# RWKV token matrices of every second pair of heads in exchanged partition halves, so that a product set addresses all four array quarters

## The chip, the cores and the metric

One core of one Trainium2 chip runs the whole program. The metric is the device time of one execution in microseconds (us); lower is better.

## The reference, cut to what matters

The program is one inference step of a two-layer network. The change lies in the RWKV-7 time mixing of the first layer, for 640 tokens (512 latent, 128 context), 8 heads of 64, in both directions of time. Per head and direction it computes

```
def rwkv7_recurrence(r, decay, kk, b, k, v, s0):
    def step(s, inp):
        r_t, w_t, kk_t, b_t, k_t, v_t = inp
        sa = einsum('dbhvk,dbhk->dbhv', s, kk_t)
        s = s * w_t[..., None, :] - sa[..., :, None] * b_t[..., None, :] + v_t[..., :, None] * k_t[..., None, :]
        return s, einsum('dbhvk,dbhk->dbhv', s, r_t)
```

All inputs and outputs are float32.

## The kernel before

The recurrence is done in chunks of 64 tokens. The 640 tokens are five tiles of 128; a **turn** (`n`, five of them) takes one tile in each direction (`e` = 0 forward, 1 backward). 128 partitions hold a pair of heads, 64 partitions each, so a direction has four pairs (`c`, RC = 4) of two chunks each (`u`): eight blocks (`j = 2c + u`, RB = 8), and a block has two independent 64x64 matrices, one in either partition half (`HALVES`).

A **product set** is 16 products of 64x64 by 64x64, one per block and half. The helper `each` (L1124) multiplies two tiles block by block, `turned` (L1134) transposes by a product with the identity `half_ident`, `added` (L1209) sums three products. Half 0 reads partitions 0 to 63 and writes partitions 0 to 63 of a PSUM bank, half 1 reads and writes 64 to 127. On the 128x128 array that is two of the four 64x64 quarters, those on the diagonal. Each float32 product appears in the trace as two MATMUL records and two LDWEIGHTS records, so a set is 32 MATMUL records.

The order of work is written out by hand, one function per engine, with semaphores between them: `rwkv_pe`, `rwkv_act`, `rwkv_dve`, `rwkv_pool`. A turn on TensorE has three stretches.

1. **Opening.** Four pair products per direction (B by A, K by A, B by R, K by R), the transposes of A, B, K, V and of the masked matrix Lm, and M by V. ScalarE copies each PSUM bank out (`LT`, `AMV`, `Btok`, `Ktok`, `Vtok`); VectorE masks the others (`MT`, `TbT`, `TkT`; L1313, L1320, L1323), makes `Lm` (`mask_level`, L1295), `XT` (L1309) and `X` (L1316).
2. **Levels.** Five rounds (`for lv in range(1, LEVELS)`) of Lm by X, XT by T1 and T1 by XT, with the low-rank products of the next turn (`prepare_lora_pe`) between them.
3. **End.** XT by AMV (L1196, 128 columns), two sets with nWG (`Phi`, `Hm`), then in two steps the new state and the output: state of both directions (first `added` loop), output of both directions (second), for step 0 and then for step 1, whose state `Sc1` VectorE makes from step 0's products (L1356).

VectorE also prepares the next turn between these: the running sums (L1053 to L1063) after `Hm`, whose exponentials ScalarE takes (L1069 to L1072), A (L1077), and, after the outputs are added into `yT` (L1365), R (L1080). Then come six small operations on the decays `em` (L1298 to L1300), `Sc` (L1303) and the first masks. GpSimd makes B and K of the next turn (L1085 to L1094) and adds the bonus; TensorE's first product of a turn waits for A, B and K of both directions (`tile_ready`).

Ahead of the turns the state is brought into place by eight transposes (L996), after them it is turned back by eight (L1393).

Of the kernel before, what the change touches and what calls it, by code (L numbers as in the profile page):

```python
# [12 lines left out]
P = 128  # L13
# [102 lines left out]
def build(nc, i, o):  # L116

    ctx = ExitStack()
    with ctx:
# [826 lines left out]
        em, em_now = [wr(RB) for _ in BOTH], [wr(RB) for _ in BOTH]  # L946
# [44 lines left out]
        def rwkv_state_pe(pe):  # L991
            pe.wait_ge(sem("lora_in"), 48)
            pe.wait_ge(sem("state_in"), 32)
            for e in range(2):
                for c in range(RC):
                    last = nc.tensor.transpose(ps[e][:, c * N:(c + 1) * N], stin[:, e, 2 * c:2 * c + 2, :].rearrange("p h k -> p (h k)"),  # L996
                                               ident[0:N, 0:N])
            last.then_inc(sem("state_turned"), 1)
# [26 lines left out]
        def bank(b):  # L1025
            return ps[b][:, :].rearrange("p (b t) -> p b t", b=RB)

# [84 lines left out]

        def rwkv_pe(pe):
            for e in BOTH:
                if e:
                    pe.wait_ge(sem("a_made"), 1)
                prepare_lora_pe(0, e, pe)
            for n in range(NT):
# [17 lines left out]

                pe.wait_ge(sem("tile_ready"), n * 4 + 4)
                for e in BOTH:
                    each(4 * e + 1, Bst[e], Ast[e]).then_inc(sem("pairs_done"), 1)
                for e in BOTH:  # L1140
                    turned(4 * e + 2, blocks_of(Ast[e])).then_inc(sem("abk_turned"), 1)
                for e in BOTH:
                    pe.wait_ge(sem("rwkv_y_kept"), n * 2 + (e + 1))
                    each(4 * e, Kst[e], Ast[e]).then_inc(sem("pairs_done"), 1)
                for e in BOTH:
                    turned(4 * e + 3, blocks_of(Bst[e])).then_inc(sem("abk_turned"), 1)
# [3 lines left out]
                for e in BOTH:  # L1150
                    pe.wait_ge(sem("abk_kept"), n * 6 + (e + 1))
                    turned(4 * e + 2, blocks_of(Kst[e])).then_inc(sem("abk_turned"), 1)
                for e in BOTH:
                    pe.wait_ge(sem("abk_kept"), n * 6 + (e + 3))
                    turned(4 * e + 3, tile_blocks(V0, n, e)).then_inc(sem("v_turned"), 1)
                for e in BOTH:
                    pe.wait_ge(sem("m_kept"), n * 2 + (e + 1))
                    pe.wait_ge(sem("r_made"), n * 2 + (e + 1))
                    each(4 * e, Bst[e], Rst[e]).then_inc(sem("pairs_done"), 1)
                for e in BOTH:  # L1160
                    pe.wait_ge(sem("abk_kept"), n * 6 + (e + 5))
                    each(4 * e + 2, Kst[e], Rst[e]).then_inc(sem("pairs_done"), 1)
# [4 lines left out]
                for lv in range(1, LEVELS):  # L1167
                    for e in BOTH:
                        pe.wait_ge(sem("x_updated"), n * 2 * (LEVELS - 1) + (2 * (lv - 1) + e + 1))
                        pe.wait_ge(sem("level_masked"), n * 2 * LEVELS + (2 * lv + e + 1))  # L1170
                        each(4 * e + 1, Lm[e], X[e]).then_inc(sem("lx_done"), 1)
                    if lv == 1 and n + 1 < NT:
                        pe.wait_ge(sem("incl_kept"), n * 4 + 2)
                        prepare_lora_pe(n + 1, 0, pe)
                    if lv == 3 and n + 1 < NT:
                        pe.wait_ge(sem("a_made"), n * 2 + 3)
                        prepare_lora_pe(n + 1, 1, pe)
                    for e in BOTH:
                        if lv == 1:
                            pe.wait_ge(sem("incl_kept"), n * 4 + (e + 3))  # L1180
                            pe.wait_ge(sem("mv_kept"), n * 2 + (e + 1))
                        pe.wait_ge(sem("lx_kept"), n * 2 * (LEVELS - 1) + (2 * (lv - 1) + e + 1))
                        pe.wait_ge(sem("xt_updated"), n * 2 * LEVELS + (2 * (lv - 1) + e + 1))
                        if lv < LEVELS - 1:
                            each(4 * e + 2, XT[e], T1[e]).then_inc(sem("x_product"), 1)
                        else:
                            each(4 * e + 3, T1[e], XT[e]).then_inc(sem("xt_product"), 1)
                    if lv < LEVELS - 1:
                        for e in BOTH:
                            each(4 * e + 3, T1[e], XT[e]).then_inc(sem("xt_product"), 1)  # L1190

                for e in BOTH:
# [6 lines left out]
                if n + 1 < NT:  # L1199
                    pe.wait_ge(sem("a_made"), n * 2 + 4)  # L1200
                for e in BOTH:
                    pe.wait_ge(sem("wg_kept"), n * 2 + (e + 1))
                    each(4 * e, nWG[e][:, :, 0:N], Btok[e])
                    each(4 * e + 3, nWG[e][:, :, 0:N], TbT[e]).then_inc(sem("phi_done"), 1)
# [6 lines left out]

                for step in range(2):
                    state = Sc1 if step else Sc
                    for e in BOTH:
                        u = 1 - e if step else e
                        pe.wait_ge(sem("sc_made" if step else "phi_kept"), n * 2 + (e + 1))
# [12 lines left out]
        def rwkv_act(act):  # L1229
            for e in BOTH:  # L1230
# [4 lines left out]
                prepare_exps_act(0, e, act)  # L1235
            for n in range(NT):
                for e in BOTH:
                    act.wait_ge(sem("pairs_done"), n * 8 + (e + 1))
                    nc.scalar.copy(LT[e], bank(4 * e + 1)).then_inc(sem("lt_kept"), 1)
                for e in BOTH:  # L1240
                    act.wait_ge(sem("abk_turned"), n * 6 + (e + 1))
                    nc.scalar.copy(AMV[e][:, :, 0:N], bank(4 * e + 2)).then_inc(sem("abk_kept"), 1)
                for e in BOTH:
                    act.wait_ge(sem("abk_turned"), n * 6 + (e + 3))
                    nc.scalar.copy(Btok[e], bank(4 * e + 3)).then_inc(sem("abk_kept"), 1)
                for e in BOTH:
                    act.wait_ge(sem("abk_turned"), n * 6 + (e + 5))
                    nc.scalar.copy(Ktok[e], bank(4 * e + 2)).then_inc(sem("abk_kept"), 1)
                for e in BOTH:
                    act.wait_ge(sem("v_turned"), n * 2 + (e + 1))  # L1250
                    nc.scalar.copy(Vtok[e], bank(4 * e + 3)).then_inc(sem("v_kept"), 1)
# [20 lines left out]
                for e in BOTH:  # L1272
                    act.wait_ge(sem("wg_done"), n * 2 + (e + 1))
# [3 lines left out]
                if n + 1 < NT:  # L1277
                    prepare_exps_act(n + 1, 1, act)

        def rwkv_dve(dve):  # L1280
# [8 lines left out]
            for n in range(NT):  # L1289
# [7 lines left out]
                for e in BOTH:  # L1297
                    nc.vector.tensor_copy(em_now[e], em[e])  # L1298
                    nc.vector.tensor_scalar(em_kept[e], sub_cols(em[e], e), keep[:, ds(n, 1)], None, ALU.mult)
                    nc.vector.tensor_tensor(em_pair[e], sub_cols(em[e], 0), sub_cols(em[e], 1), ALU.mult)  # L1300
# [10 lines left out]
                for e in BOTH:  # L1311
                    dve.wait_ge(sem("pairs_done"), n * 8 + (e + 3))
                    nc.vector.tensor_tensor(MT[e], bank(4 * e), bc(strict[:, e * N:(e + 1) * N], [P, RB, N], 1), ALU.mult).then_inc(sem("m_kept"), 1)  # L1313
                for e in BOTH:
# [3 lines left out]
                for e in BOTH:  # L1318
                    dve.wait_ge(sem("pairs_done"), n * 8 + (e + 5))
                    nc.vector.tensor_tensor(TbT[e], bank(4 * e), bc(within[:, e * N:(e + 1) * N], [P, RB, N], 1), ALU.mult).then_inc(sem("incl_kept"), 1)  # L1320
                for e in BOTH:
                    dve.wait_ge(sem("pairs_done"), n * 8 + (e + 7))
                    nc.vector.tensor_tensor(TkT[e], bank(4 * e + 2), bc(within[:, e * N:(e + 1) * N], [P, RB, N], 1), ALU.mult).then_inc(sem("incl_kept"), 1)  # L1323
# [22 lines left out]
                for e in BOTH:  # L1346
                    dve.wait_ge(sem("phi_done"), n * 2 + (e + 1))
                    nc.vector.tensor_tensor(Phi[e], bank(4 * e), eye, ALU.add)
                    nc.vector.tensor_tensor(Hm[e], bank(4 * e + 3), Rst[e], ALU.add)
# [9 lines left out]
                for e in BOTH:  # L1359
                    dve.wait_ge(sem("state_made"), n * 4 + (e + 3))  # L1360
                    nc.vector.tensor_tensor(S[e], sub(bank(4 * e), 1 - e), bc(sub_cols(em_now[e], 1 - e), [P, RC, N], 2), ALU.mult)
                for e in BOTH:
                    y = yT[:, :, tokens_of(n, e)]
                    dve.wait_ge(sem("y_done"), n * 2 + (e + 1))
                    nc.vector.tensor_tensor(y, y, ps[4 * e + 3][:, :].rearrange("p (c t) -> p c t", c=RC), ALU.add)  # L1365
# [22 lines left out]
        def rwkv_end_pe(pe):  # L1388
            end_step_pe(pe, 0, lambda c: pairs, lambda c: yT[:, c, :])

            for e in range(2):
                for c in range(RC):
                    last = nc.tensor.transpose(ps[4 + e][0:N, c * P:(c + 1) * P], S[e][:, c, :], ident)  # L1393
# [1005 lines left out]
```

## Time and profile before

| | us |
|---|---|
| three runs: median (lowest to highest) | 2692.62 (2692.33 to 2698.26) |
| profiled execution: its own time | 2691.81 |
| profiled execution: span | 2689.8 |
| TensorE busy in the span | 2448.0 (91%) |
| VectorE / ScalarE / GpSimd busy | 601.4 / 536.0 / 217.9 |
| the five turns, first product to the last output | 457.55 to 796.26 |

The span runs from the first to the last instruction; the execution's own time is 2.0 us longer. A busy time is the union of an engine's records. A matrix product's record is longer than the time after which the next may start, so rates are taken from counts over a stretch and not from the mean of one record. The granted TensorE clock is given as a share of 2.4 GHz: 1.00 is 2.4, 0.50 is 1.2.

### The profile page before, as it was taken

What the parts mean: (1) busy time and instruction counts of PE and PEld (TensorE: products, weight loads), DVE (VectorE), ACT (ScalarE), POOL (GpSimd) and SP (SyncE); (2) the same over time, 40 slices, a digit from 0 to 9 for tenths busy, and PEclk for the clock granted to TensorE, in tenths of its full rate; (3) what the DMA queues carried; (4) which work ended last, traced back from release to release, by engine and by line L of the source; (5) the groups of instructions that cost most, each with busy time, mean ns of one, the idle gap of its engine ahead of it and who ended that gap; (6) DMA issues with size and microseconds to landing.
All of it is one profiled execution on the core that took longest, in us unless ns stands there. A gap on an engine that the chain in (4) does not pass through costs nothing.

```text
span 2689.8 us, 74227 instructions
## 1 busy us (share of the span) xinstructions
PE 2448.0 (91%) x34058; PEld 1706.7 (63%) x34058; DVE 601.4 (22%) x1164; ACT 536.0 (20%) x1037; POOL 217.9 (8%) x243
## 2 busy tenths in 40 slices
PE   5899985999999769999999899998794999999998
PEld 3555564999994466777666345457453777766654
DVE  1113456666652330000000010106315000000001
ACT  3111043444421310000000036114413000000000
POOL 2000020333300010000000000003001000000000
PEclk8999997999999889999999999999896999999999
DMA  7665300000012269999999311110014999999970
GB/s 282 191 216 180 132 1 14 4 4 4 4 44 68 108 248 373 397 397 396 396 394 392 115 50 47 48 63 32 16 58 159 353 392 397 396 394 394 396 274 39
DMA packets 173468, 529.19 MB, mean 197 GB/s; under 512 B 23124, under 2 KB 27888, under 8 KB 173296
## 3 DMA queue, kind: packets, MB, share of 16 engines
q1 hardware_dynamic: 158688, 489.45, 48.1%
q10 hardware_dynamic: 10336, 24.21, 3.1%
q0 software_dynamic: 4272, 12.91, 1.4%
q8 instruction: 147, 2.41, 0.4%
q14 instruction: 25, 0.20, 0.0%
HBM read 506.75 MB, written 11.40 MB: 193 GB/s over the span
## 4 chain that ended last, share of the span: by engine, by line
PE 68%; issue 16%; DMA 5%; DVE 3%; ACT 2%; POOLq 1%; ACTq 1%; DVEq 1%; POOL 1%; SPq 0%
PE ps L1710 19%; PE ps L1725 17%; PE ps L1124 7%; PE ps L458 4%; PE ps L1840 4%; DMA big<-w_exp_down 3%; PE ps L1209 2%; PE ps L1912 2%; PE ps L1134 2%; PE ps L1908 2%; PE ps L460 1%; PE ps L830 1%; PE ps L438 1%; PE ps L1703 1%; PE ps L1196 1%
## 5 line engine op out<-in xcount | busy, mean ns | idle before, releaser
L1710 PE MATMUL ps<-rs,ring 128*64 128x80 f32 x12288 | 441.8, 233 | 5.8 <-issue 5.5
L1710 PEld LDWEIGHTS ps<-rs,ring 128*64 128x64 f32 x12288 | 429.9, 137 | 23.9 <-issue 23.0
L1811 DVE TENSOR_TENSOR big<-big,ps 128x320 f32<-128x320 f32 x64 | 28.3, 483 | 993.8 <-PE ps L1725 954.8
L1725 PE MATMUL ps<-big 128*80 128x512 f32 x512 | 226.4, 595 | 1.9 <-DMA big<-w_exp_down 1.5
L1725 PE MATMUL ps<-ring,big 128*80 128x512 f32 x512 | 225.0, 592 | 2.4 <-DVE big L1811 2.4
L555 PE MATMUL ps<-hT,ring 128*128 128x512 f32 x336 | 176.1, 606 | 11.1 <-ACTq L602 11.1
L1124 PE MATMUL ps<-big 64*64 64x64 f32 x5440 | 166.5, 219 | 16.9 <-DVEq L1095 16.9
L1781 ACT COPY big<-ps 80x512 f32<-80x512 f32 x64 | 34.1, 582 | 711.0 <-PE ps L1725 711.0
L1124 PEld LDWEIGHTS ps<-big 64*64 64x64 f32 x5440 | 163.1, 136 | 18.2 <-DVEq L1095 17.2
L1725 PEld LDWEIGHTS ps<-ring,big 128*80 128x80 f32 x512 | 76.6, 150 | 145.9 <-issue 141.8
L1725 PEld LDWEIGHTS ps<-big 128*80 128x80 f32 x512 | 74.3, 150 | 131.5 <-issue 129.8
L1710 PE MATMUL ps<-rs,big 128*64 128x80 f32 x4096 | 148.2, 233 | 1.6 <-issue 1.6
L1710 PEld LDWEIGHTS ps<-rs,big 128*64 128x64 f32 x4096 | 144.5, 137 | 2.6 <-issue 2.4
L1912 PE MATMUL ps<-hT,ring 128*128 128x512 f32 x256 | 132.0, 597 | 0.8 <-issue 0.8
L1840 PE MATMUL ps<-hT,big 128*128 128x512 f32 x256 | 115.1, 602 | 3.4 <-DMA prompt_rows<-big 3.4
L556 PEld LDWEIGHTS ps<-hT,ring 128*128 128x128 f32 x336 | 64.4, 192 | 81.6 <-issue 81.6
L458 PE MATMUL ps<-hT,ring 128*128 128x512 f32 x192 | 100.4, 605 | 10.5 <-issue 9.3
L1743 POOL COPY rs<-big 128x640 f32 (+1 forms) x32 | 23.1, 722 | 928.9 <-PE ps L1710 928.9
L1913 PEld LDWEIGHTS ps<-hT,ring 128*128 128x128 f32 x256 | 48.6, 190 | 61.2 <-issue 61.2
L1840 PEld LDWEIGHTS ps<-hT,big 128*128 128x128 f32 x256 | 48.6, 195 | 59.8 <-issue 55.3
L1774 ACT ACTIVATE big<-ps 128x320 f32<-128x320 f32 x64 | 24.5, 435 | 288.8 <-PE ps L1710 288.8
L1908 PE MATMUL ps<-ring,hT 128*128 128x512 f32 x160 | 69.2, 593 | 0.3 <-issue 0.3
(392 smaller groups left out, 3002.1 us busy)
## 6 DMA issues: line engine op xcount, KB each, us to landing
ring<-w_exp_up SPq DMA_DIRECT2D x124, 1024.0 KB, 10.8
ring<-w_exp_gate SPq DMA_DIRECT2D x68, 1024.0 KB, 12.1
big<-w_exp_down SPq DMA_DIRECT2D x64, 1024.0 KB, 11.3
ring<-w_exp_down SPq DMA_DIRECT2D x64, 1024.0 KB, 11.5
big<-w_exp_gate SPq DMA_DIRECT2D x60, 1024.0 KB, 10.6
big<-w_ada SPq DMA_DIRECT2D x22, 2048.0 KB, 8.7
ring<-w_in_odd SPq DMA_DIRECT2D x6, 2048.0 KB, 8.9
big<-big ACTq DMA_DIRECT2D x32, 256.0 KB, 6.4
```

Source lines behind the costliest of these rows:

```text
L458: nc.tensor.matmul(ps[2 * pair][:, :], blocks[s][:, k, j * P:(j + 1) * P], rhs(k, 0, TS), start=(k == 0), stop=(k == KC - 1))
L555: nc.tensor.matmul(ps[2 * pair][:, :], w, hT[:, k, 0:TS], start=(k == 0), stop=(k == KC - 1))
L556: last = nc.tensor.matmul(ps[2 * pair + 1][:, 0:TP], w, hT[:, k, TS:T], start=(k == 0), stop=(k == KC - 1))
L1124: last = nc.tensor.matmul(ps[b][hf, j * N:(j + 1) * N], lhs[hf, j, :], rhs[hf, j, :], start=True, stop=True)
L1134: last = nc.tensor.matmul(ps[b][hf, j * N:(j + 1) * N], x[j][hf], half_ident[hf, :], start=True, stop=True)
L1209: last = nc.tensor.matmul(ps[b][hf, j * N:(j + 1) * N], lhs[hf], rhs[hf], start=(t == 0), stop=(t == len(terms) - 1))
L1710: last = nc.tensor.matmul(ps[2 * m + j // 4][a:a + HALF, (j % 4) * SLOTS:(j % 4 + 1) * SLOTS], ex_blocks[ex_slot(q)][:, k % 2, j * P + a:j ...
L1725: last = nc.tensor.matmul(ps[4 + f][0:SLOTS, :], hid[:, k, :], ex_blocks[ex_slot(q)][:, k % 2, f * W:(f + 1) * W], start=(k == 0), stop=(k ...
L1840: nc.tensor.matmul(ps[b][:, :], outS[:, a, c * P:(c + 1) * P], turnS[:, a, :], start=(a == 0), stop=(a == E // 2 - 1))
L1908: last = nc.tensor.matmul(ps[2 * pair][:, :], hT[:, k, tile * P:(tile + 1) * P], blocks[s][:, k, :], start=(k == 0), stop=(k == KC - 1))
L1912: nc.tensor.matmul(ps[2 * pair][:, :], w, hT[:, k, 0:TS], start=(k == 0), stop=(k == KC - 1))
L1913: last = nc.tensor.matmul(ps[2 * pair + 1][:, 0:TP], w, hT[:, k, TS:T], start=(k == 0), stop=(k == KC - 1))
```

## The change

For odd pairs `c` the two heads' token matrices (what has tokens on its partitions, or results from such) exchange partition halves. Even pairs keep the diagonal quarters, odd pairs read half g and write half 1 - g, which are the other two quarters. The new helper `across` goes through four places `k` and takes in each an even pair (f = 0, bank b) and an odd pair (f = 1, bank b + 1), so four products in a row address four quarters. `added_across` does it for the outputs. The sets that go through them, per direction and turn: four pair products, the transposes of A, B, K and V, and the outputs (three sets). `each`, `turned` and `added` keep the others: Lm's transpose, M by V, the levels, XT by AMV, `Phi`, `Hm` and the states.

Since a set now fills half of two banks, the readers take both (`spread`), and the results stand in order of place (`placed`). The pair products, transposes and outputs share banks in a new order: the transposes of A, B, K and V all use banks 4e+2 and 4e+3, the pair products banks 4e and 4e+1, each waiting until the one before has been read. Three things are added: R is moved to exchanged halves by a set of products with the identity and copied to `Hm` by ScalarE before XT by AMV (`r_turned`, `r_placed`); the decays `em` of odd pairs cross halves by two products of 64x4 and two copies per direction (`place_em_pe`, `place_em_act`), for the next turn ahead of the step 1 outputs; and the state goes in and out by 16 products in place of eight transposes each.

On TensorE, the opening of the first turn. Before (L1124 is `each`, L1134 `turned`; two sets of 16 per pair of rows):

```order
L1124 MATMUL ps<-big 64x64 [waits tile_ready]
L1124 MATMUL ps<-big 64x64 x31
L1134 MATMUL ps<-big 64x64 x32
L1124 MATMUL ps<-big 64x64 [waits rwkv_y_kept]
L1124 MATMUL ps<-big 64x64 x15
L1124 MATMUL ps<-big 64x64 [waits rwkv_y_kept]
L1124 MATMUL ps<-big 64x64 x15
L1134 MATMUL ps<-big 64x64 x32
L1134 MATMUL ps<-big 64x64 [waits level_masked]
```

and with the change (L1175 is `across`, L1164 `turned`):

```order
L1175 MATMUL ps<-big 64x64 [waits em_placed,tile_ready]
L1175 MATMUL ps<-big 64x64 x15
L1175 MATMUL ps<-big 64x64 [waits em_placed]
L1175 MATMUL ps<-big 64x64 x15
L1175 MATMUL ps<-big 64x64 [waits rwkv_y_kept]
L1175 MATMUL ps<-big 64x64 x15
L1175 MATMUL ps<-big 64x64 [waits rwkv_y_kept]
L1175 MATMUL ps<-big 64x64 x15
L1164 MATMUL ps<-big 64x64 [waits level_masked]
```

Eight sets stood ahead of the one that waits for the mask of Lm; four are left. K by A and the transpose of B now follow it.

On VectorE, the opening of the first turn. Before:

```order
L1303 TENSOR_TENSOR big<-big 128x256 x2
L1295 TENSOR_TENSOR big<-big 128x512 [waits lt_kept] x2
L1309 TENSOR_TENSOR big<-big 128x512 x2
L1313 TENSOR_TENSOR big<-ps,big 128x512 [waits pairs_done] x2
```

and with the change, where L1388 is `X`, L1369 `mask_level`, and L1392 `MT` (L1313 before):

```order
L1378 TENSOR_TENSOR big<-big 128x256 x2
L1369 TENSOR_TENSOR big<-big 128x512 [waits lt_kept] x2
L1384 TENSOR_TENSOR big<-big 128x512 x2
L1388 TENSOR_TENSOR big<-big,ps 128x512 [waits x_product]
L1369 TENSOR_TENSOR big<-big 128x512
L1388 TENSOR_TENSOR big<-big,ps 128x512 [waits x_product]
L1369 TENSOR_TENSOR big<-big 128x512
L1392 TENSOR_TENSOR big<-ps,big 128x512 [waits pairs_done] x2
```

`MT` went behind both `X` and their masks.

On TensorE, the start of the end stretch with the change (L1250 is XT by AMV, L1196 before); the first two rows are the new set of R, for both directions:

```order
L1175 MATMUL ps<-ring0,big 64x64 [waits a_made]
L1175 MATMUL ps<-ring0,big 64x64 x31
L1250 MATMUL ps<-big 64x128 [waits r_placed,xt_updated]
L1250 MATMUL ps<-big 64x128 x15
```

Before, XT by AMV waited for `xt_updated` alone, and `a_made` was waited for behind it.

The diff, cut to its core:

```
+        def spread(b):
+            return banks[:, b * 512:(b + 2) * 512].rearrange("p (f r) -> p f r", f=2)[:, :, 0:4 * N].rearrange("p f (k t) -> p f k t", k=4)
...
+        def place_em_pe(turn, pe):
+            for e in BOTH:
+                pe.wait_ge(sem("exps"), turn * 2 + (e + 1))
+                odd_pairs = em[e].rearrange("p (a f u) -> p f a u", a=2, f=2)[:, 1]
+                for g in range(2):
+                    last = nc.tensor.matmul(ps[4 * e + 1][HALVES[1 - g], 0:4].rearrange("p (a u) -> p a u", a=2), half_ident[HALVES[g], :],
+                                            odd_pairs[HALVES[g]], start=True, stop=True)
+                last.then_inc(sem("em_crossed"), 1)
...
+                def across(b, lhs, rhs, apart=1):
+
+                    for k in range(4):
+                        for f in range(2):
+                            for g in range(2):
+                                last = nc.tensor.matmul(ps[b + apart * f][HALVES[g ^ f], k * N:(k + 1) * N], half_ident[HALVES[g], :] if lhs is None else lhs[f][k][HALVES[g]],
+                                                        half_ident[HALVES[g], :] if rhs is None else rhs[f][k][HALVES[g]], start=True, stop=True)
+                    return last
...
                 for e in BOTH:
-                    each(4 * e + 1, Bst[e], Ast[e]).then_inc(sem("pairs_done"), 1)
-                for e in BOTH:
-                    turned(4 * e + 2, blocks_of(Ast[e])).then_inc(sem("abk_turned"), 1)
+                    if n:
+                        pe.wait_ge(sem("sc_made"), n * 4 + (e - 1))
+                    pe.wait_ge(sem("em_placed"), n * 2 + (e + 1))
+                    across(4 * e, b_of[e], a_of[e]).then_inc(sem("pairs_done"), 1)
...
+                for e in BOTH:
+                    across(4 * e, None, r_of[e], 2).then_inc(sem("r_turned"), 1)
                 for e in BOTH:
                     pe.wait_ge(sem("xt_updated"), n * 2 * LEVELS + (2 * (LEVELS - 1) + e + 1))
+                    pe.wait_ge(sem("r_placed"), n * 2 + (e + 1))
...
+                    if step and n + 1 < NT:
+                        place_em_pe(n + 1, pe)
                     for e in BOTH:
                         u = 1 - e if step else e
-                        for c in range(RC):
-                            j = 2 * c + u
-                            last = added(4 * e + 3, j, [(Vtok[e][:, j], TkT[e][:, j]), (nWG[e][:, j, N:P], TbT[e][:, j]), (state[e][:, c], Hm[e][:, j])])
+                        for a in range(2):
+                            k = 2 * a + u
+                            last = added_across(4 * e + 2, k, [(two(Vtok[e], k), two(TkT[e], k)), (two(nWG[e][:, :, N:P], k), two(TbT[e], k)),
+                                                               ([state[e][:, 2 * f + a] for f in range(2)], two(Hm[e], k))])
...
                 for e in BOTH:
+                    act.wait_ge(sem("r_turned"), n * 2 + (e + 1))
+                    for f in range(2):
+                        last = nc.scalar.copy(Hm[e][:, 4 * f:4 * f + 4, :], ps[4 * e + 2 * f][:, 0:4 * N].rearrange("p (k t) -> p k t", k=4))
+                    last.then_inc(sem("r_placed"), 1)
```

## Rows read from the trace of the kernel before

**Rows 1.** Windows of three stretches; columns: us, engines' busy us, clock, DMA.

```profile
457.50:463.60 6.10, 6.05 (x114) 6.05 (x116) 5.15 (x14) 1.77 (x3) 0.00 (x0) 0.50 0.01 4
595.90:614.60 18.70, 18.70 (x648) 18.70 (x645) 13.33 (x25) 6.48 (x11) 2.73 (x2) 1.00 0.02 4
614.60:645.00 30.40, 30.40 (x934) 30.02 (x930) 20.86 (x31) 16.46 (x34) 13.58 (x11) 1.00 0.02 4
```

**Rows 2.** Timeline, TensorE, one turn: start us, duration us, then line and operands.

```profile
595.93 2.03 PE L1124 MATMUL ps<-big 64*64 64x64 f32 x64
...
614.60 2.03 PE L1124 MATMUL ps<-big 64*64 64x64 f32 x64
```

**Rows 3.** Window of line L351 alone; groups of the list by line.

```profile
37.10:40.50 3.40, 3.40 (x128) 3.27 (x132) 1.00 0.08 8
...
L1710 PE MATMUL ps<-rs,ring 128*64 128x80 f32 x12288 | 441.8, 233 | 5.8 <-issue 5.5
...
L1725 PE MATMUL ps<-big 128*80 128x512 f32 x512 | 226.4, 595 | 1.9 <-DMA big<-w_exp_down 1.5
...
L810 PE MATMUL ps<-big 64*128 64x384 f32 x32 | 7.9, 573 | 0.5 <-ACTq L868 0.5
```

**Rows 4.** Timeline, TensorE, end of a turn; last row: window, line L1209.

```profile
577.20 3.74 PE L1196 MATMUL ps<-big 64*64 64x128 f32 x64
...
584.50 0.28 PE L1209 MATMUL ps<-ring 64*64 64x64 f32 x4
...
584.50:595.93 11.43, 11.41 (x384) 11.27 (x384) 1.00 0.02 4
```

**Rows 5.** Timeline, ScalarE: state-in copies, the turn's end, the next turn's first copy.

```profile
425.99 0.65 ACT L1003 COPY big<-ps 128x256 f32<-128x256 f32 x2 [0.82 <-PE ps L996]
...
576.00 1.15 ACT L1047 ACTIVATE ring<-ps,parB 128x128 f32<-128x128 f32 x4
...
597.08 0.59 ACT L1239 COPY big<-ps 128x512 f32<-128x512 f32 x1 [6.11 <-PE ps L1124]
```

**Rows 6.** Timeline, VectorE and GpSimd between two turns.

```profile
589.25 0.76 DVE L1356 TENSOR_TENSOR big<-ps,big 128x256 f32<-128x256 f32 x2
...
592.80 1.27 POOL L1094 TENSOR_TENSOR big<-ring 128x512 f32<-128x512 f32 x1
```

**Rows 7.** Timeline, VectorE, start of a turn.

```profile
596.15 0.69 DVE L1365 TENSOR_TENSOR hT<-hT,ps 128x512 f32<-128x512 f32 x1 [0.71 <-PE ps L1209]
...
600.64 1.29 DVE L1295 TENSOR_TENSOR big<-big 128x512 f32<-128x512 f32 x2
602.03 1.30 DVE L1309 TENSOR_TENSOR big<-big 128x512 f32<-128x512 f32 x2
```

**Rows 8.** Windows of a later stage with waits; columns as in rows 1.

```profile
1852.70:1856.20 3.50, 1.71 (x8) 1.53 (x9) 2.26 (x5) 3.25 (x8) 0.00 (x0) 1.00 0.00 0
1869.80:1873.30 3.50, 0.21 (x1) 0.21 (x2) 2.77 (x5) 2.10 (x5) 1.10 (x1) 1.00 0.02 7
1873.30:1876.70 3.40, 3.40 (x9) 2.69 (x9) 3.21 (x5) 1.34 (x4) 1.90 (x1) 0.50 0.00 0
```

**Rows 9.** Timeline, first turn: TensorE, then VectorE.

```profile
457.55 3.68 PE L1124 MATMUL ps<-big 64*64 64x64 f32 x64 [16.89 <-DVEq L1095]
...
461.02 3.19 PE L1134 MATMUL ps<-big 64*64 64x64 f32 x64
...
478.98 2.03 PE L1124 MATMUL ps<-big 64*64 64x64 f32 x64
...
461.75 1.28 DVE L1295 TENSOR_TENSOR big<-big 128x512 f32<-128x512 f32 x2
```

**Rows 10.** Timeline, VectorE and TensorE around the stage's two edges.

```profile
426.34 4.33 DVE L1006 MEMSET hT<- 128x5120 f32 x1 [1.26 <-PEq L186]
...
787.17 0.43 DVE L1356 TENSOR_TENSOR big<-ps,big 128x256 f32<-128x256 f32 x1 [1.20 <-PE ps L1209]
...
801.10 1.04 PE L1393 MATMUL ps<-ck,big 128*64 128x128 f32 x8
```

More of the change, by code:

```diff
@@ L945, in build @@
         half, go_on = wr(RB), wr(1)
-        em, em_now = [wr(RB) for _ in BOTH], [wr(RB) for _ in BOTH]
+        em, em_placed, em_now = ([wr(RB) for _ in BOTH] for _ in range(3))
         em_kept, em_pair = [wr(RC) for _ in BOTH], [wr(RC) for _ in BOTH]
@@ L995, in rwkv_state_pe @@
                 for c in range(RC):
-                    last = nc.tensor.transpose(ps[e][:, c * N:(c + 1) * N], stin[:, e, 2 * c:2 * c + 2, :].rearrange("p h k -> p (h k)"),
-                                               ident[0:N, 0:N])
+                    for h in range(2):
+                        q = 2 * (c % 2) + c // 2
+                        last = nc.tensor.matmul(ps[e][HALVES[h ^ (c % 2)], q * N:(q + 1) * N], stin[:, e, 2 * c + h, :], ident[0:N, 0:N], start=True, stop=True)
             last.then_inc(sem("state_turned"), 1)
@@ L1158, in rwkv_pe @@
                     pe.wait_ge(sem("r_made"), n * 2 + (e + 1))
-                    each(4 * e, Bst[e], Rst[e]).then_inc(sem("pairs_done"), 1)
+                    across(4 * e, b_of[e], r_of[e]).then_inc(sem("pairs_done"), 1)
                 for e in BOTH:
                     pe.wait_ge(sem("abk_kept"), n * 6 + (e + 5))
-                    each(4 * e + 2, Kst[e], Rst[e]).then_inc(sem("pairs_done"), 1)
+                    across(4 * e + 2, heads(tile_blocks(V0, n, e)), None).then_inc(sem("v_turned"), 1)
+                for e in BOTH:
+                    pe.wait_ge(sem("incl_kept"), n * 4 + (e + 1))
+                    across(4 * e, k_of[e], r_of[e]).then_inc(sem("pairs_done"), 1)
                 for e in BOTH:
@@ L1198, in rwkv_pe @@
                     last.then_inc(sem("wg_done"), 1)
-                if n + 1 < NT:
-                    pe.wait_ge(sem("a_made"), n * 2 + 4)
                 for e in BOTH:
                     pe.wait_ge(sem("wg_kept"), n * 2 + (e + 1))
-                    each(4 * e, nWG[e][:, :, 0:N], Btok[e])
-                    each(4 * e + 3, nWG[e][:, :, 0:N], TbT[e]).then_inc(sem("phi_done"), 1)
+                    each(4 * e + 1, nWG[e][:, :, 0:N], Btok[e])
+                    each(4 * e + 2, nWG[e][:, :, 0:N], TbT[e]).then_inc(sem("phi_done"), 1)
                 def added(b, j, terms):
@@ L1210, in added, with added_across, two @@
                     return last
+                def added_across(b, k, terms):
+                    for t, (lhs, rhs) in enumerate(terms):
+                        for f in range(2):
+                            for g in range(2):
+                                last = nc.tensor.matmul(ps[b + f][HALVES[g ^ f], k * N:(k + 1) * N], lhs[f][HALVES[g]], rhs[f][HALVES[g]],
+                                                        start=(t == 0), stop=(t == 2))
+                    return last
+                def two(x, k):
+                    return [x[:, 4 * f + k] for f in range(2)]
                 for step in range(2):
@@ L1215, in rwkv_pe @@
                         u = 1 - e if step else e
-                        pe.wait_ge(sem("sc_made" if step else "phi_kept"), n * 2 + (e + 1))
+                        pe.wait_ge(sem("sc_made" if step else "phi_kept"), n * (4 if step else 2) + (e + 1))
                         for c in range(RC):
@@ L1272, in rwkv_act @@
                 for e in BOTH:
+                    act.wait_ge(sem("r_turned"), n * 2 + (e + 1))
+                    for f in range(2):
+                        last = nc.scalar.copy(Hm[e][:, 4 * f:4 * f + 4, :], ps[4 * e + 2 * f][:, 0:4 * N].rearrange("p (k t) -> p k t", k=4))
+                    last.then_inc(sem("r_placed"), 1)
+                for e in BOTH:
                     act.wait_ge(sem("wg_done"), n * 2 + (e + 1))
@@ L1392, in rwkv_end_pe @@
                 for c in range(RC):
-                    last = nc.tensor.transpose(ps[4 + e][0:N, c * P:(c + 1) * P], S[e][:, c, :], ident)
+                    q = 2 * (c % 2) + c // 2
+                    for h in range(2):
+                        last = nc.tensor.matmul(ps[4 + e][0:N, c * P + h * N:c * P + (h + 1) * N], S[e][:, q, :],
+                                                ident[:, HALVES[h ^ (c % 2)]], start=True, stop=True)
             last.then_inc(sem("state_turned"), 1)
```

69 lines of the change are left out of this document (45 added, 24 removed).

## The prediction

> **What bounds the kernel now.** I read the windows by stage first, then TensorE's timeline, then the engines it waits for. Inside the turns TensorE never stops: 18.70 us busy of 18.70 in the opening of a turn and 30.40 of 30.40 in the levels, at the full clock [rows 1]. An opening is 20 product sets from 595.93 to 614.60 [rows 2], so a set of 32 records takes 18.67 / 20 = 0.933 us, 58 ns for every two records, one in either quarter of the diagonal. The reader should see that nothing else limits this: VectorE is busy 13.33 of the 18.70 us and ScalarE 6.48 [rows 1]. TensorE's time is thus the stage's time, but the cover is thin: VectorE makes its first mask of the turn only at 600.64, 4.7 us after the first product [rows 2, 7], and that wait is hidden by sets that the change shortens or moves.
>
> **Does a quarter cost nothing beside another?** The trace has no stretch with four 64x64 quarters, so the price of an `across` set has to be bounded. A full row of 512 columns takes 226.4 / 512 = 0.442 us, so 64 columns stream in 55 ns, hardly less than the 58 seen for two records. Line L351, which writes four groups of partitions, starts 128 records of 128 columns in 3.40 us, 26.6 ns each, where one alone streams 110 ns: four go on at once, from the same input partitions. L1710 does the same with two groups and 64-column weight loads: 36 ns a record where 80 columns stream 69. L810 reads the two halves of the input and writes the same 128 output partitions, in two banks: 7.9 us / 32 = 247 ns where 384 columns stream 331 [rows 3]. Both directions of sharing are there, not their product. The low bound of a set is therefore 0.467 us (four records in 58 ns), the high bound 0.933 (no gain). I take 0.467, since each of the two sharings alone costs nothing in its row.
>
> The Trainium skill, "TensorE: Matmul & The Clock Gate", Part 3, says that a weight load overlaps running products only where its row group differs; two of the four quarters share theirs. By that rule a set would stay near 0.933. L1710's 36 ns, with both column groups on all rows, speaks against it [rows 3].
>
> **The change, part by part.** Times from here count from the start of the state products, 584.50, called P.
>
> *Set of R, before XT by AMV.* The `a_made` it waits for ends at 577.15, XT by AMV began at 577.20 [rows 4, 5]. R of both directions takes 577.2 to 578.15. ScalarE starts 0.22 after the first direction's set (as 597.08 stands to 596.86 [rows 2, 5]) and copies two pieces of 256 columns, priced at 0.65 by the copies at 425.99 [rows 5]: done at 578.55. XT by AMV then starts at 578.65, **1.45 us later**; the second direction's copies lie under the first's product. P moves with it.
>
> *Outputs and states.* Twelve sets took 11.43 us [rows 4]. State step 0 stays: 3.03 with its short wait. Step 0's outputs shrink from 2.8 to 1.4 and end at P + 4.43. There a wait appears: `Sc1` of the first direction is ready only at 589.25 + 0.43 = P + 5.18 [rows 6, 10], as VectorE does the running sums first. State step 1 runs 5.25 to 8.05, the crossing of `em` 0.2 (the exponentials are ready by about P + 6.5, since GpSimd starts behind them), step 1's outputs to 9.65. B and K of the next turn are ready when GpSimd's L1094 ends, 594.07 = P + 9.57, some 0.1 later with its drain [rows 6]. The turn starts at **P + 9.75** instead of 11.43.
>
> *The opening.* Product B by A and the transpose of A are four short sets: to P + 11.6. Lm's transpose then waits for the mask. VectorE adds the last outputs 0.22 after them, and from that addition (596.15) to the end of the first mask (600.64 + 0.69) takes 5.18 [rows 7]: 9.65 + 0.22 + 5.18 = 15.05. **TensorE idles 3.5 us.** From there: Lm 15.1 to 16.95, transposes of B to 17.9. VectorE ends `XT` 2.69 after the mask began [rows 7], at 17.05, then makes X, mask, X, mask in steps of 0.6 to 0.65, to 19.6. K by A goes at 17.9 and, behind the second X, at 19.1 to 19.55; K's transposes to 20.5; `MT` is kept at 20.2 and 20.85; B by R 20.5 to 21.4, V to 22.3, K by R (behind `TbT`, 21.85 and 22.5) to 23.3, M by V, two full sets, to 25.1. The levels start at **P + 25.1**; before, at 614.60 - 584.50 = 30.1. So a boundary gains 5.0 - 1.45 = 3.5 us. The levels themselves keep 30.40: their sets stay.
>
> *The clock.* In a later stage a stretch with TensorE busy 0.21 of 3.50 us was followed by one at 0.50 of the clock (1.2 GHz); one with 1.71 of 3.50 was not [rows 8]. An idle 3.5 us lies between. I take a fall at nearly every boundary and a return soon after: at half the clock two sets take 461.02 - 457.55 = 3.47 us [rows 9], so Lm's pair takes 3.4 instead of 1.87, of which VectorE's chain absorbs about 0.8: 0.7 lost. A boundary nets 2.8, four of them **11.2 us**.
>
> *First turn.* From 457.55 to 478.98 before [rows 9], beginning at half the clock [rows 1]. The masks start at 461.75 as now [rows 9]; Lm at 462.5, at half the clock to 465.9, then B's transposes, K by A at 467.8. With the clock back about then, `MT` ends at 469.6 and the levels follow 4.3 later as above: 473.9. Half of that clock's return is open, so I take **4.5** of the 5.
>
> *Last turn.* The wait for R costs 1.45, the outputs give back 2.8; `Sc1` is ready at 787.60 [rows 10], under the products: **1.35**.
>
> *State in and out.* Eight transposes become 16 products. Inbound they lie under VectorE's 4.33 us fill [rows 10]; without that cover they cost 1 us. Outbound they stand on TensorE's path: eight took 0.87, 32 records one after another take 1.85: **-1.0**.
>
> *At nothing:* the `em` copies (ScalarE waited 6.11 us for its first copy of a turn [rows 5]); reading two banks in place of one, as the elements stay 512. If that cost an operation 0.17 us (half-size operations take 0.43 each [rows 10] against 0.69 [rows 7]), five on the chain would take 0.9 a turn; both ends go into the range.
>
> Sum: 11.2 + 4.5 + 1.35 - 1.0 = 16.0 us. The profiled execution took 2691.81, 0.8 under the median of the runs: **2676 us**.
>
> **The rivals.**
>
> *The issue of records is the limit.* No stretch starts records faster than the 26.6 ns of L351 [rows 3]; a short set needs 14.6. If 26.6 is as fast as they can be issued, a set takes 0.85 us. Outputs end at P + 11.13, the mask at 16.5, and behind Lm come twelve sets of 0.85 and M by V: levels at P + 30.5, 0.4 later than now, and R delays P by 1.85. Each boundary loses 2.25, the last turn 1.35, the state out 1.0: **2703, slower**. It decides above about 0.7 us a set, where gain and loss meet. Against it: L351's rate is explained by its columns. Chance 0.15. The Trainium skill, same page, "Back-to-back issue gap", gives a floor of about 25 ns from start to start for small products; by that, an estimate, a set would take 0.8 us. The trace neither reaches nor breaks it.
>
> *The quarters don't overlap.* A set stays 0.933, and only the new waits and sets remain: 3.8 a boundary, 2711. Against it all of [rows 3]. Chance 0.05.
>
> *Partial overlap,* 0.7 us a set: levels at P + 28, R 1.65, so 0.45 a boundary gained and eaten by the state out: 2690. Chance 0.10.
>
> *The clock stays low* through most of each opening: 2.5 lost a boundary instead of 0.7 and 2 more in the first turn: 2685. For it: sparse work after the gap. Against: from K by A on TensorE is nearly dense. Chance 0.10.
>
> **How the numbers follow.** The forecast has 0.60: 2671 (no fall of the clock, first turn 6) to 2681 (two-bank reads at their bound). A difference under 0.3%, 8 us, can't be told from none. Faster: the forecast and half of the low clock, 0.65; same: the other half, the partial case and a milder issue limit, 0.17; slower: the rest, 0.18. The range takes in the forecast, the low clock and the partial case with their bounds, 2668 to 2697.
>
> **What would show it.** `across` sets with 32 records in about 0.47 us; an idle stretch of some 3.5 us on TensorE after the transposes of A, ended by VectorE's first mask, and the clock at 0.50 behind it; XT by AMV waiting about 0.5 us for ScalarE; turns of 64 to 65 us instead of 67.8. Wrong it would be if 32 records took 0.8 us or more, if K by A rather than Lm waited longest, or if the next turn's B and K came later than 9.7 us after the state products began.

## The result, and the profile after

The changed kernel takes 2695.93 us (median of 20 runs, 2689.82 to 2702.50), the kernel before 2689.53 us beside it (20 runs, 2685.02 to 2698.26): a ratio of 1.0025, 95% interval 1.0017 to 1.0033. So it is slower by a quarter of a per cent, 6.4 us, where 2676 was forecast. The time lies inside the range, near its upper end, but the forecast had the direction wrong. The profiled execution took 2697.08 us.

The page, engines and the queue of instructions, changed kernel (each engine: busy us, share of the span, instructions):

```profile
span 2695.3 us, 75088 instructions
...
PE 2425.0 (90%) x34466; PEld 1674.0 (62%) x34466; DVE 602.8 (22%) x1164; ACT 542.6 (20%) x1077; POOL 219.0 (8%) x243
...
q8 instruction: 150, 2.46, 0.4%
```

TensorE is busy 23 us less than before (2448.0) and the span is 5.5 us longer, so its idle time over the span grew by some 28 us. Window of the turns, from the first pair product to the pass that follows them (columns as in [rows 1]):

```profile
457.54:802.98 345.44, 306.49 (x11041) 298.79 (x11041) 210.47 (x346) 133.46 (x278) 101.48 (x88) 0.97 0.02 4
```

Before, the same stretch (457.55 to 796.44) took 338.89 us, 337.87 of them busy. The array was relieved as meant, by 31 us here; but where TensorE idled 1 us it now idles 39, and the turns take 6.55 us more. Starts of XT by AMV, in us:

| turn | 1 | 2 | 3 | 4 | 5 |
|---|---|---|---|---|---|
| before | 509.38 | 577.20 | 645.00 | 712.82 | 776.62 |
| after | 509.73 | 578.65 | 649.66 | 719.08 | 784.44 |

The turns that should have shrunk from 67.8 to 64 or 65 us take 68.9, 71.0, 69.4 and, the last, 65.4 (63.8 before). At the last XT by AMV the kernel is 7.8 us late.

TensorE's timeline in one opening, changed kernel (it answers to [rows 2]; at the end of a line the idle time before it, and what released it):

```profile
526.71 0.73 PE L1175 MATMUL ps<-big 64*64 64x64 f32 x33
528.23 1.62 PE L1175 MATMUL ps<-big 64*64 64x64 f32 x95 [0.79 <-issue]
532.74 2.02 PE L1164 MATMUL ps<-big 64*64 64x64 f32 x62 [2.88 <-DVE big L1369]
...
536.72 1.63 PE L1175 MATMUL ps<-big 64*64 64x64 f32 x96 [0.50 <-DVE big L1388]
538.17 0.65 PE L1175 MATMUL ps<-ring,big 64*64 64x64 f32 x32
540.25 0.69 PE L1175 MATMUL ps<-ring,big 64*64 64x64 f32 x32 [1.44 <-issue]
540.77 1.11 PE L1175 MATMUL ps<-big 64*64 64x64 f32 x64
541.70 0.65 PE L1175 MATMUL ps<-ring,big 64*64 64x64 f32 x32
543.98 0.69 PE L1175 MATMUL ps<-ring,big 64*64 64x64 f32 x32 [1.63 <-DVE big L1398]
544.50 2.03 PE L1154 MATMUL ps<-ring,big 64*64 64x64 f32 x64
546.36 2.35 PE L1154 MATMUL ps<-big 64*64 64x64 f32 x64
```

Read two things. From 540.77 to 541.70 two sets pass in 0.93 us, 0.467 each: the four quarters do run at once. But the sets come in groups with stops between them, and the reason given is "issue": TensorE waited for nothing that the profile shows. Before, an opening had no stop at all [rows 1].

TensorE's waits over the five turns, up to 800 us, changed kernel (us in total, times, longest):

```profile
PE ps L1175 <- issue: 15.7, 13, 1.9
PE ps L1164 <- DVE big L1369: 10.6, 5, 2.9
...
PE ps L1250 <- ACT big L1343: 1.9, 4, 0.7
...
PE ps L1154 <- issue: 2.4, 2, 1.4
...
PE ps L1269 <- issue: 0.9, 2, 0.6
```

The forecast knew the second and the third of the rows shown: 3.5 us a turn for VectorE's first mask, about 0.5 us for ScalarE's copy of R. The 19.0 us of "issue" (15.7 + 2.4 + 0.9; with one of 0.97 at 801.63, in the last outputs, 20.0) it did not know. Even the 1.63 us at 543.98, put down to VectorE, are such a stop: K by R of the second direction waits there for that direction's `TbT`, and VectorE had kept it at 541.02 + 0.69 = 541.71:

```profile
541.02 0.69 DVE L1395 TENSOR_TENSOR big<-ps,big 128x512 f32<-128x512 f32 x1 [1.44 <-PE ps L1175]
```

The last view is that of the DMA queues, for 533 to 545 us of the same opening, 40 slices of 0.3 us:

```profile
DMA  0020000000000000100000000000200000000000
GB/s 0 0 55 0 0 0 0 0 0 0 0 0 0 0 0 0 55 0 0 0 0 0 0 0 0 0 0 0 55 0 0 0 0 0 0 0 0 0 0 0
...
q8 instruction: 3, 0.05, 1.6%
```

A DMA queue named "instruction" is at work all the time; the flood below shows that it feeds TensorE. Three packets start in these 12 us, in the slices from 533.6, 537.8 and 541.4, and the two stops end at 540.25 and 543.98, some 2.5 us after the second and the third of them.

**Theory F** from this: TensorE's instructions come in blocks, one every 3.6 us or so; a set is 64 instructions (32 loads, 32 products), and four sets of 0.467 us use up in 1.9 us a block that is replaced only after 3.6. **Theory W**, the rival: the changed order and its new waits took back what the quarters gave. **Theory I**: each instruction has a floor of its own, the rival of the prediction.

The counts fit F: between the ends of the stops at 540.25 and 543.98 lie 32 + 64 + 32 = 128 products, with their loads one block. Counted from the start of the trace, TensorE has begun 5413, 5796 and 5924 products when it goes on at 528.23, 540.25 and 543.98, and in the next opening 7704, 7960 and 8087 at 599.38, 608.69 and 612.70: within each opening a multiple of 128 further, to within one record. Where it waited for a mask the count has no such distance (5508 at 532.74).

### The profile page after: what moved, and what is told of

Same layout as the page of the kernel before. It is cut to its first block, busy times and chain, and to the rows that moved or that the text cites. A ratio compares the mean times of both kernels' runs of the same rounds, so it can differ in the third digit from the quotient of the medians.

```text
span 2695.3 us, 75088 instructions
## 1 busy us (share of the span) xinstructions
PE 2425.0 (90%) x34466; PEld 1674.0 (62%) x34466; DVE 602.8 (22%) x1164; ACT 542.6 (20%) x1077; POOL 219.0 (8%) x243
## 4 chain that ended last, share of the span: by engine, by line
PE 66%; issue 17%; DVE 5%; DMA 4%; ACT 2%; POOLq 1%; DVEq 1%; ACTq 1%; POOL 1%; SPq 0%
PE ps L1788 19%; PE ps L1803 17%; PE ps L1154 6%; PE ps L458 4%; PE ps L1918 4%; DMA big<-w_exp_down 2%; PE ps L1990 2%; PE ps L1986 2%; PE ps L1175 1%; PE ps L460 1%; PE ps L830 1%; PE ps L438 1%; PE ps L1781 1%; PE ps L1250 1%; PE ps L1261 1%
## 5 line engine op out<-in xcount | busy, mean ns | idle before, releaser
L1154 PE MATMUL ps<-big 64*64 64x64 f32 x4800 | 145.3, 218 | 1.0 <-issue 1.0
L1154 PEld LDWEIGHTS ps<-big 64*64 64x64 f32 x4800 | 142.7, 134 | 2.4 <-issue 1.4
```

Source lines behind the costliest of these rows:

```text
L1154: last = nc.tensor.matmul(ps[b][hf, j * N:(j + 1) * N], lhs[hf, j, :], rhs[hf, j, :], start=True, stop=True)
```

## The experiments

**The same order without the exchange.** Everything of the change but the crossing:

```diff
-   ps[b + apart * f][HALVES[g ^ f], ...]      # across
+   ps[b + apart * f][HALVES[g], ...]
-   ps[b + f][HALVES[g ^ f], ...]              # added_across
+   ps[b + f][HALVES[g], ...]
```

and likewise for `em` and the states' way in and out.

> The changed kernel with its order, waits, banks and instruction count as they are, but every token matrix, em and state stays in its own partition half, so that a product set uses two array quarters at a time instead of four. Theory F (TensorE's instructions reach it in blocks of 256 about every 3.6 us, so that sets of 64 instructions cannot go faster than about 0.9 us each for long): sets go back from 0.467 to 0.933 us, the stops whose releaser the profile calls issue all but go, and the time stays within 2698 to 2710 us (per turn the R set's 1.9 us of array and its wait). Theory W (the changed order and its new waits cost what was lost, the quarters gained what was forecast): the 22 sets and the outputs of a turn take 13 us longer, of which the waits hide at most 4: 2740 to 2760 us.

Measured: 2707.14 us (6 runs), ratio to the kernel before 1.0061 (1.0048 to 1.0075): F. TensorE's timeline of the same opening, and all its waits of 1 us or more over the turns:

```profile
531.61 3.90 PE L1175 MATMUL ps<-big 64*64 64x64 f32 x128
537.06 2.08 PE L1164 MATMUL ps<-big 64*64 64x64 f32 x64 [1.55 <-DVE big L1369]
538.97 5.77 PE L1175 MATMUL ps<-big 64*64 64x64 f32 x192
544.57 2.03 PE L1175 MATMUL ps<-ring,big 64*64 64x64 f32 x64
```

```profile
PE ps L1164 <- DVE big L1369: 6.2, 4, 1.5
PE ps L1175 <- DVEq L1109: 4.3, 1, 4.3
```

Six sets take 544.57 - 538.97 = 5.60 us, 0.933 each, and no stop called issue is left. The same window of the turns as above:

```profile
458.89:815.48 356.59, 349.33 (x11040) 346.38 (x11041) 210.08 (x346) 135.80 (x278) 100.98 (x88) 0.99 0.02 4
```

The changed kernel is busy 42.8 us less than this one (306.49 against 349.33) and its turns are only 11.15 us shorter (345.44 against 356.59): nearly three quarters of what the quarters gave came back as 31.7 us of idle time. Some two thirds of that are stops of the supply, the rest are the new waits of the changed order, the mask's above all (10.6 us against 6.2). So W has a share, the smaller one. Its 2740 to 2760 was reckoned a little high: a turn has 18 short sets and 6 for the outputs, 11 us of array time and not 13, which would make it 2732 to 2752, still far from the 2707.14 measured.

**What an instruction stream does by itself.** The changed kernel with 2048 tiny instructions ahead of its first turn (512 products of 4 columns, each two products and two loads in the trace; their results are never used):

```diff
+   for i in range(512):
+       nc.tensor.matmul(ps[2 + i % 2][HALVES[i % 2], 0:4][0:4], half_ident[HALVES[i % 2], 0:4],
+                        half_ident[HALVES[i % 2], 0:4], start=True, stop=True)
```

> The changed kernel with 512 products of 4 by 4 put once ahead of its first turn, results unused: 2048 instructions with next to no array work, to be read in the trace. F: they go in bursts with a few ns between instructions and stops of over 1 us between bursts, 256 instructions per 3.5 to 3.7 us on the average, 28 us or more in all. Theory I (a floor on each instruction, 13 to 14 ns): an even stream, no stops, 27 to 30 us in all. If neither limits, they are through in under 15 us. The kernel's time is longer by what does not fit ahead of the first turn's matrices, 0 to 30 us.

Measured: 2714.44 us, a single run. TensorE's timeline:

```profile
451.80 2.84 PE L1149 MATMUL ps<-big 64*4 64x4 f32 x214
456.18 1.75 PE L1149 MATMUL ps<-big 64*4 64x4 f32 x128 [1.54 <-issue]
459.91 1.75 PE L1149 MATMUL ps<-big 64*4 64x4 f32 x128 [1.98 <-issue]
463.64 1.75 PE L1149 MATMUL ps<-big 64*4 64x4 f32 x128 [1.98 <-issue]
467.37 1.75 PE L1149 MATMUL ps<-big 64*4 64x4 f32 x128 [1.98 <-issue]
471.10 1.75 PE L1149 MATMUL ps<-big 64*4 64x4 f32 x128 [1.98 <-issue]
474.55 1.75 PE L1149 MATMUL ps<-big 64*4 64x4 f32 x128 [1.71 <-issue]
478.00 0.69 PE L1149 MATMUL ps<-big 64*4 64x4 f32 x42 [1.71 <-issue]
478.62 2.62 PE L1177 MATMUL ps<-big 64*64 64x64 f32 x86
```

and a window over five of these bursts, with the weight loads in the second pair, and the queue of instructions from 453.6 to 475.7:

```profile
456.18:474.55 18.37, 8.74 (x641) 8.28 (x640) 3.48 (x11) 0.00 (x0) 0.00 (x0) 0.50 0.02 5
```

```profile
q8 instruction: 6, 0.10, 2.0%
```

This is the limit, bare. The first 214 products with their loads, about 430 instructions, go without a stop: that much was waiting. Then every burst is 128 products and 128 loads, one block of 256, and the bursts start 3.73 us apart, the last two steps 3.45: 14 ns an instruction on the average (18.37 us / 1281). Inside a burst an instruction takes no more than 1.75 us / 256 = 7 ns, at half the clock. An even floor (I) would show no stops. Six packets on the queue stand beside the six full bursts. The whole flood took 478.62 - 451.80 = 26.8 us, a little under the 28 that F gave, since its start came out of what was waiting; the 27 to 30 us of I would have fitted nearly as well, so it is the stops that decide.

**Another form of the exchange, as a control.** A block goes to the half of its pair's parity (and to the bank of its own half) instead of to the other half:

```diff
-   ps[b + apart * f][HALVES[g ^ f], ...]
+   ps[b + apart * g][HALVES[f], ...]
```

> Control for the next run: the changed kernel with another exchange of halves of the same cost. A token matrix goes to the partition half of its pair's parity and to the column group of its half, where the changed kernel does it the other way about; same quarters, same sets, same instruction count on TensorE. All theories: the changed kernel's time within 0.15%, 2692 to 2700 us. If the quarters did not overlap in this form, sets of 0.933 us in the trace.

Measured: 2695.44 us (12 runs), 1.0017 (1.0008 to 1.0025), the changed kernel's time; 18.3 us of "issue" ahead of `across`, 21.7 in all. `added_across`, `em` and the state's way in and out were turned over in the same way.

**Fewer instructions for the same transposes.** In that form both halves of a transposed block land in one partition half, side by side, so one call can do it (ScalarE's four copies of them then read one bank):

```diff
+   def stood(b, x):
+       for k in range(4):
+           for f in range(2):
+               out = ps[b][HALVES[f], :].rearrange("p (g k t) -> p g k t", g=2, k=4)[:, :, k]
+               last = nc.tensor.matmul(out, x[f][k], ident.rearrange("p (g t) -> p g t", g=2), start=True, stop=True)
+       return last
-   across(4 * e + 2, a_of[e], None)           # and B, K, V
+   stood(4 * e + 2, a_of[e])
```

> The control with the eight transposing sets of a turn (A, B, K, V for both directions) written as 8 calls of 128 rows by 64 columns against a 128-wide identity, where they were 16 calls of 64 by 64: 32 instructions in a set where there were 64, 256 fewer in a turn, with the same columns of array work and the same waits. F: one block of instructions less in each turn, 3.6 us, 14 to 18 us in all: 2678 to 2682 us; the stops called issue fall from 16 us to about a quarter. W: nothing, 2692 to 2700 us. If a transposing set of this form takes 0.9 us for itself (the array not shared by two of them), F gives 2682 to 2696 us.

Measured: 2692.29 us (12 runs), 1.0009 (0.9999 to 1.0019): 3.2 us less than the control, not 14 to 18. The stops fell about as F said, from 21.7 us to 6.9 in all, but the array's time did not stay:

```profile
PE ps L1178 <- issue: 4.4, 3, 2.0
...
PE ps L1280 <- issue: 2.2, 3, 1.4
```

```profile
533.57 1.97 PE L1187 MATMUL ps<-ck,big 128*64 128x128 f32 x32
535.47 1.16 PE L1178 MATMUL ps<-ring,big 64*64 64x64 f32 x64
```

The waits are those over the turns, the timeline that of one opening: two transposing sets (L1187) take 535.47 - 533.57 = 1.90 us, 0.95 each, where `across` takes 0.467. The 128-wide identity has two zero quarters, and its zeros stream like its ones; "the same columns of array work" in the expectation was wrong. Eight sets of +0.48 us gave back in every turn what 256 saved instructions brought. The bound given for that case, 2682 to 2696, holds the time. Longer sets alone also make stops fewer, as in the first experiment, so the stops do not decide here. The time does: 19 us more of array work in five turns (40 sets) and half of the instructions in them came out no slower than the control. By how much the stops fell is uncertain: the control's traced execution took 2702.42 us, 7.0 over its median, this one's 2685.59, 6.7 under.

**Earlier masks.** VectorE's small steps on `em` and `Sc` behind X, the second masks and `MT` instead of ahead of the first masks:

```diff
-       nc.vector.tensor_copy(em_now[e], em_placed[e])
    ...
-       nc.vector.tensor_tensor(Sc[e], S[e], bc(em_kept[e], [P, RC, N], 2), ALU.mult)
        mask_level(e, 0)
    ...
        nc.vector.tensor_tensor(placed(MT[e]), spread(4 * e), each_place(strict[:, e * N:(e + 1) * N]), ALU.mult).then_inc(sem("m_kept"), 1)
+       nc.vector.tensor_copy(em_now[e], em_placed[e])
    ...
+       nc.vector.tensor_tensor(Sc[e], S[e], bc(em_kept[e], [P, RC, N], 2), ALU.mult)
```

> The changed kernel with VectorE's seven small steps on em and Sc moved from ahead of a turn's first masks to behind the second masks and X, so that the first mask starts about 1.3 us earlier; TensorE's instructions stay as they are. Theory W (the wait for the first mask, 10.6 us in five turns, is what ate the gain): 1.3 us less in each turn, 6 us in all: about 2689 us. Theory F (what is missing behind the mask is instructions): the wait shrinks, the stops called issue grow by about as much, 2692 to 2697 us.

Measured: 2691.24 us (12 runs), 1.0005 (0.9996 to 1.0015), between W's number and F's range; the time alone decides nothing. TensorE's waits over the turns:

```profile
PE ps L1175 <- issue: 19.0, 15, 2.0
...
PE ps L1154 <- issue: 3.1, 5, 1.1
...
PE ps L1269 <- issue: 2.2, 3, 1.0
...
PE ps L1164 <- issue: 1.7, 2, 1.3
...
PE ps L1164 <- DVE big L1369: 1.0, 2, 0.8
```

The wait for the mask fell by 9.6 us, from 10.6 to 1.0, and the stops called issue rose from 20.0 to 26.2 (with a last row of 0.2), by 6.2. In this trace about two thirds of what the masks gave turned into waiting for instructions. The traced execution took 2686.80 us, 4.4 under the median, so the share is not exact. F was a little too strict; a likely reason, not tried by itself, is that a wait for something else does not always leave time to store instructions.

**Both together, with half of the transposes in one call.** The control's form, the earlier masks, and `stood` for B and K alone (A and V over four quarters):

> The other exchange (the control) with that order on VectorE and, of the four kinds of transposing sets, B's and K's in one call of 128 rows, A's and V's over four quarters. In the run with all four in one call the stops fell from 18.3 to 4.4 us but each such set took 0.93 us. F: 128 instructions fewer in a turn, 1.8 us of supply, while the 1.9 us more of array work fit into what are stops now; with the masks earlier 2 to 3 us a turn under the changed kernel, 2682 to 2688 us, and the stops called issue about half of the changed kernel's. W: the 1.9 us of array work come on top, less 1.3 for the mask: 2696 to 2699 us.

Measured: 2685.57 us (12 runs), 0.9983 (0.9972 to 0.9994): faster than both kernels. The stops called issue are 8.6, 2.3 and 2.3 us, 13.2 in all where the changed kernel has 20.0: more than the half that was expected.

```profile
PE ps L1178 <- issue: 8.6, 7, 2.2
...
PE ps L1280 <- issue: 2.3, 4, 1.1
PE ps L1157 <- issue: 2.3, 3, 1.7
```

**R behind each direction's last XT product,** in the kernel of the run before (ScalarE's copy reads the same banks).

```diff
    each(4 * e + 3, T1[e], XT[e]).then_inc(sem("xt_product"), 1)
+   if n + 1 < NT:
+       pe.wait_ge(sem("w_made"), n * 2 + 4)
+   across((0, 5)[e], None, r_of[e], (2, 1)[e]).then_inc(sem("r_turned"), 1)
    ...
-   for e in BOTH:
-       across(4 * e, None, r_of[e], 2).then_inc(sem("r_turned"), 1)
```

> The kernel of the run before, with each direction's R set issued right behind that direction's last XT product and in banks that are free there, so that XT by AMV of the first direction waits neither for the copies of R nor for the last update. Each turn 0.5 us less than the run before, 2 to 3 us in all; the wait of XT by AMV for ACT's copy of R (1.9 us in five turns) goes. If TensorE's instructions are the limit there too, under 1 us.

Measured: 2683.27 us (12 runs), 0.9975 (0.9964 to 0.9985), 6.6 us under the kernel before and 12 to 13 under the changed one. It is 2.3 us under the run before, as expected, though the two intervals overlap. That the wait is gone shows in the timeline: the last R set starts at 572.87 and XT by AMV follows at 573.34, one set later, with no idle time. The stops called issue are 14.6 us there, 13.2 in the run before: a part of what the wait gave went to them.

```profile
572.87 0.64 PE L1178 MATMUL ps<-ring,big 64*64 64x64 f32 x30
573.34 3.69 PE L1262 MATMUL ps<-big 64*64 64x128 f32 x64
```

## Why the prediction was wrong

**What bounds the kernel now: read too narrowly.** TensorE never stops in a turn, and that was taken to mean that the array sets the time. The stream of instructions was running at nearly the same pace: 64 instructions in 0.933 us are 14.6 ns each, and the flood gives 14 ns at best for any length of time. Relieving the array alone could gain next to nothing in a stretch longer than the store of instructions. The DMA queues of the profile before gave a hint of it: a queue named "instruction" with 147 packets.

**The price of a set: right for a set, wrong for a stretch.** 0.467 us was taken from [rows 3], and it is what two adjacent sets take, 0.93 us. The rival of no overlap and that of a partial one fall with it. The Trainium skill, "TensorE: Matmul & The Clock Gate", Part 3, lets a weight load overlap running products only where the row group differs. The measured 0.467, two row groups shared by two quarters each, goes against it here.

**The failed step** is in the part on the opening: Lm's pair, the twelve short sets behind it and M by V were summed at array time with VectorE's steps beside them, 10.0 us from Lm (P + 15.1) to the levels (P + 25.1). The supply of instructions stood in the sum at nothing. Measured from the state products at 517.01: the next turn starts at P + 9.70 (forecast 9.75), Lm at 532.74 = P + 15.7 (forecast 15.1; the two first masks took 2.35 us together where [rows 7] has 1.29), the levels at 546.36 = P + 29.35 (forecast 25.1; before, 30.1). Lm to the levels takes 13.6 instead of 10.0, and 3.1 of these 3.6 us are the stops at 540.25 and 543.98. With R's 1.56 us, some stops in the levels and the clock (below), the 3.5 us gained a boundary turn into a loss of 1.1 to 3.2 us a turn.

**The sum.** For the turns a gain of 11.2 + 4.5 + 1.35 = 17.05 us was forecast and a loss of 6.55 found, a miss of 23.6. Against it stand 21.6 us of stops: the 20.0 called issue and the 1.63 at 543.98. This is a comparison of sizes and no exact account, since a stop also covers waits that would have come without it.

**The rivals.** "The issue of records is the limit" gave 2703 and 0.15. Its direction and most of its size are what happened, its mechanism is not: there is no floor of 26.6 ns for a pair, since short sets start products 14.6 ns apart and the flood's bursts start them every 13 to 14 ns. The Trainium skill, same page, "Back-to-back issue gap", has a floor of about 25 ns from start to start for small products. Neither stretch here respects it, both of products that change between parts of the array. The limit is a supply by blocks, which lets about 430 instructions through without a stop and then holds the rest to 14 ns. That is also why the loss is smaller than 2703 said.

**The clock** was forecast to fall at nearly every boundary. Windows of the changed kernel behind three of the idle stretches (clock third from the end):

```profile
604.00:606.00 2.00, 2.00 (x66) 2.00 (x66) 1.91 (x5) 0.00 (x0) 0.00 (x0) 0.50 0.00 0
...
613.20:616.50 3.30, 3.30 (x106) 3.30 (x96) 1.39 (x2) 0.59 (x1) 0.00 (x0) 0.50 0.02 5
...
674.00:676.00 2.00, 2.00 (x110) 2.00 (x109) 1.91 (x4) 0.23 (x1) 0.00 (x0) 1.00 0.03 8
```

It fell in two of the four openings: twice in the one at 600, behind the wait for the mask and again behind a stop, and once near 743; not in those at 530 and 671. The opening with two falls belongs to the longest turn, 71.0 us; how much of its length is the clock's was not separated.

**First turn:** 4.5 forecast, 1.2 found (the first of the next turn's low-rank products at 479.73 against 480.94); stops again, 3.5 us of "issue" in that opening. **Last turn:** the outputs were to give back 2.8 us and the R set to cost 1.45. XT by AMV, which stands behind the R set, to the pass after the turns shrank from 19.82 to 18.54 us, so the outputs gave 1.28; the stop at 801.63 took 0.97. With R's 1.60 the last turn lost 0.3 us where 1.35 was to be gained. **Set of R:** XT by AMV starts 1.56 us behind the R set's start (577.09 to 578.65), 0.39 of it waiting for ScalarE, and 1.60 in the last turn; forecast 1.45. **State out:** 1.0 forecast; from the first product of the pass after the turns to its first sum over heads it takes 11.45 us instead of 10.12, 1.3 lost. The start of the turn, P + 9.70, the set of R and the state's way out, with few short sets in a row, were right; the first and the last turn missed by stops like the boundaries.

## What to carry to other kernels

When many tiny products bind a stage, count its instructions as well as its array time: here TensorE got 256 instructions every 3.5 to 3.7 us at best, and work that uses them faster than that stops, whatever the array could do. Look at the instruction queue among the DMA queues and at waits put down to "issue" before pricing a faster set by its own time; a burst within the store tells nothing about a stretch. Once instructions are the limit, the useful moves are those that save instructions where there are stops to fill, even at some array time, and those that take waits away where instructions have been stored.

## What the runs showed of the hardware

- TensorE's instructions arrive in blocks of 256, by DMA: bursts of 128 products with 128 loads 3.73 or 3.45 us apart, with a first burst of about 430 from store. What sets the period of a block (one fetch at a time, its latency), and whether other DMA traffic lengthens it, was not tried.
- Four 64x64 quarters take four products together: 32 in 0.467 us, 14.6 ns each. A product with 128 rows by 64 columns against 128 columns took 1.90 us / 32 = 59 ns, about half of the 110 ns that 128 columns alone take at the 0.442 us for 512 of [rows 3]: two column halves overlap, but the zeros of the identity are not free.
- Idle stretches on TensorE that ended at 602.12 (2.17 us), 612.70 (1.93) and 742.09 (2.83) were followed by a fall of the clock to 0.50; those that ended at 532.74 (2.88) and 673.14 (1.70) were not.
